# A hybrid encoder block on one core: the residual kept as two half-width tables, with each expert block's rows added by two scatters and the down product taken one half of its columns at a time

## The chip, the core and the metric

The kernel runs on one core of a Trainium2 chip. The metric is the time of one execution on the device in microseconds (us); lower is better. Five engines work side by side, each through its own instructions in order: PE (TensorE, matrix products), ACT (ScalarE), DVE (VectorE), POOL (GpSimd) and SP (SyncE, which here only issues transfers). PEld is PE's loading of the stationary matrix. Sixteen DMA engines carry out the transfers that SP, ACT and POOL issue. Engines wait for each other through semaphores.

## The reference

What is computed is one layer on 2048 tokens of 1024 columns: a mixer (gated recurrence and long convolutions), a residual addition, a mixture of 32 experts of which each token uses two, a second residual addition, and a final norm. The part that the change touches:

```
x = x + y_cat @ w_out[l]
x = x + _hier_moe(_rmsnorm(x, norm_ffn_g[l]), ...)      # top 2 of 32 experts per token

def expert_block(args):                  # 128 tokens of one expert
    xblk, e = args
    a = jax.nn.silu(xblk @ w1[e]) * (xblk @ w3[e])
    return a @ w2[e]                     # 512 -> 1024 columns

y = jnp.zeros((n_tok, d)).at[sorted_tok].add(yb[dest] * sorted_gate[:, None])
return _rmsnorm(x, norm_final_g)
```

## The kernel before

The program is a row of phases (filters and first norm, input projection and recurrence, long convolutions, `output_projection`, `route`, `experts`, `final_norm`). Between two phases all engines meet, and SP clears the next phase's semaphores one by one and adds 16 to those that start from a base (`PhaseSemaphores.begin`); then the phase starts.

`output_projection` works on 16 tiles of 128 tokens. For a tile DVE writes the new residual `X2`, ACT issues its store to the scratch table `X2` in DRAM (L1309) and only then squares the tile for the next norm (L1312); the norm gives `h`, which PE turns and multiplies for the router's logits.

`route` sorts the tokens by expert into blocks of 128. In this run there are 48 blocks for the 32 experts: each expert has one or two.

`experts` loops over experts and, within one, over its blocks (`per_block`: the count is read from memory, so every engine runs the same loops by itself). Float32 products are made of three products of rounded parts (`products`, L1670: high by high, high by low, low by high). For block B:

- SP loads the weights of the next expert, 12 slabs of 128 x 1024 (8 slabs as two transfers of 2 KB rows, 4 slabs of `exp_w2` with 4 KB rows), each as soon as DVE has finished with the slab of the expert before (L1617).
- ACT and DVE split the weights in pairs of slabs (`split_w`: `wh_hi`/`wh_lo` for the up products, `wy_hi`/`wy_lo` for the down product). Each of these engines does so before its own work on the first block of that expert, in its instruction order.
- PE makes the up products of block B (48 matmuls into banks `p1` and `p3`), turns the gathered rows of block B+1 (`px`), makes the down product `y` of the block before (24 matmuls into two banks `pyy0` and `pyy1`, 512 columns each), and turns the activations of the block just done (`pta`).
- ACT in its body: `a_hi` from `pta`, then `store_y` (both halves of the block's result, scaled by the gates, into `yb`), then the silu of the up product, then `x_hi`.
- POOL in its body: `scatter` (wait for `y_evac`, copy the 128 row numbers to `curspot`, add the rows of `yb` to table `X2` by an indirect transfer with add, L1638), then `gather_after` (rows of block B+2 into `xg`, L1625), then `added` (wait until the scatter has landed, tell ACT by `y_added`). ACT overwrites `yb` only after that, so no two scatters are under way at once.

After the loops PE makes one more down product, ACT stores two blocks and POOL scatters them one after the other (L1654 on). `final_norm` loads table `X2` in 16 transfers of 512 KB from SP (L1825), squares and scales each tile on ACT and DVE, and stores each in two transfers (L1831).

Of the kernel before, what the change touches and what calls it, by code (L numbers as in the profile page):

```python
# [11 lines left out]
P = 128  # L12
# [1083 lines left out]
def output_projection(nc, dram, LG, w_hi, w_lo, ident):  # L1096

    NL = N_GROUPS + N_EXP
    with ExitStack() as ctx:
# [171 lines left out]
        def _(act):  # L1271
# [27 lines left out]
            for t in range(NT):  # L1299
# [9 lines left out]
                act.dma_start(dram["X2"][t], X2[:, q, :]).then_inc(x2_out[q], 16)  # L1309
# [8 lines left out]
            for q in range(4):  # L1318
                act.wait_ge(x2_out[q], 16 * (NT // 4))

        @block.vector
        def _(dve):
# [26 lines left out]
            for t in range(NT):  # L1349
# [23 lines left out]
                at_least(dve, x2_out[q], 16 * (t // 4))  # L1373
# [178 lines left out]
def experts(nc, dram, nblk, idx, spot, weight, ident):  # L1552
# [5 lines left out]
    with ExitStack() as ctx:  # L1558
# [18 lines left out]
        pool_passed, act_passed = sem("pool_passed"), sem("act_passed")  # L1577
        xg_in, y_out = sem("xg_in", 0), sem("ye_out", 0)
# [5 lines left out]
        spot_ready, y_added = sem("spot_ready"), sem("y_added")  # L1584
        idx_ready, trx, xhi_ready, xlo_ready = sem("idx_ready"), sem("trx"), sem("xhi_ready"), sem("xlo_ready")
        s_ready, a_ready, tra, ahi_ready, alo_ready, y_done, y_evac = (
            sem(n) for n in ("s_ready", "a_ready", "tra", "ahi_ready", "alo_ready", "y_done", "y_evac"))
# [32 lines left out]
        def _(pool):  # L1620
# [24 lines left out]
            rows = dram["X2"].rearrange("t p d -> (t p) d")  # L1645
# [3 lines left out]
            def body(e, B):  # L1649
                scatter(B)  # L1650
                gather_after(B + 1)
                added(B)

            B = per_block(pool, "pool", body)  # L1654
            for last in range(2):
                scatter(B + last)
# [5 lines left out]
        def _(pe):  # L1662
# [23 lines left out]
            def y(B):  # L1686
# [241 lines left out]
```

## Time and profile before

| | |
|---|---|
| median of 3 runs | 2351.66 us (2348.36 to 2352.35) |
| the profiled execution's own time | 2352.69 us |
| its span in the profile | 2350.9 us |
| phase `experts`, first instruction | 1380.1 us of the span |
| phase `final_norm`, first transfer issued | 2305.95 us of the span |
| granted TensorE clock, mean | 0.946 of full speed |

A row of the profile gives an engine, a line of the kernel, an operation, the tiles it writes and reads (buffer numbers left out, so `pyy` is both banks), its count and its duration. Idle time in front of an instruction is put down to whatever ended it. "PE busy" counts overlapping matmuls, so it can read 100% while the step from one matmul to the next is shorter than the duration given for one.

### The profile page before, as it was taken

The page shows a single profiled execution, that of the slowest core. Times are in us where ns is not written, and L with a number is a line of the kernel's source. Part 1 is how long each engine was busy: PE and PEld are TensorE (multiplying, and loading weights), DVE is VectorE, ACT ScalarE, POOL GpSimd, SP SyncE. Part 2 cuts the span into 40 slices and gives each one's busy share as a digit, 9 for nine tenths or more (in the row PEclk, how much of TensorE's full clock was granted, in tenths as well). Part 3 has the DMA queues.
Part 4 walks back from the last instruction along what each step waited for, and adds up shares of the span by engine and source line. Part 5 has one row for each costly group of instructions (what it writes and reads, how often), then busy time and mean ns, then how long its engine had stood idle before and what let it go on. Part 6 is the DMA issues. An engine that isn't in the chain of part 4 may idle for free. (4 is left out here: it accounts for less than half of the span.)

```text
span 2350.9 us, 30834 instructions
## 1 busy us (share of the span) xinstructions
PE 2076.8 (88%) x9101; PEld 1502.8 (64%) x9102; DVE 1217.1 (52%) x1106; ACT 1142.7 (49%) x1335; POOL 341.4 (15%) x310
## 2 busy tenths in 40 slices
PE   3997999999999497869999459999999999999980
PEld 2655787777666131227778348888787788888870
DVE  7553223224666454654444443555868755654643
ACT  6771222226565232333332134566868766665643
POOL 0560000000000130220000002221211121221220
PEclk9998999999999798989999759999999999999995
DMA  5561213221110698756443157776989987886847
GB/s 186 163 222 58 72 36 99 90 72 39 38 39 18 261 367 324 274 203 230 166 135 103 53 190 221 268 268 217 383 300 375 384 285 227 292 287 195 286 132 303
DMA packets 239628, 462.15 MB, mean 197 GB/s; under 512 B 24896, under 2 KB 87332, under 8 KB 235173
## 3 DMA queue, kind: packets, MB, share of 16 engines
q1 hardware_dynamic: 201798, 375.23, 43.9%
q0 software_dynamic: 14400, 52.44, 9.3%
q10 hardware_dynamic: 23360, 33.56, 4.4%
q8 instruction: 43, 0.70, 0.1%
q14 instruction: 27, 0.22, 0.0%
HBM read 346.86 MB, written 114.29 MB: 196 GB/s over the span
## 5 line engine op out<-in xcount | busy, mean ns | idle before, releaser
L1670 PE MATMUL p<-wh_hi,x_hi 128*128 128x512 f32 x768 | 308.5, 402 | 11.0 <-DVE wh_lo L1792 10.9
L1792 DVE TENSOR_TENSOR wh_lo<-w_raw,wh_hi 128x2048 fp32r<-128x2048 f32 x128 | 284.8, 2287 | 51.6 <-ACT wh_hi L1757 49.8
L1670 PE MATMUL p<-wh_lo,x_hi 128*128 128x512 f32 x768 | 303.8, 396 | 0.0
L1670 PE MATMUL p<-wh_hi,x_lo 128*128 128x512 f32 x768 | 303.7, 395 | 0.0
L495 PE MATMUL pj<-h_hi,wp_hi 128*128 128x512 f32 x640 | 256.5, 401 | 12.4 <-DVE wp_lo L672 12.4
L495 PE MATMUL pj<-h_lo,wp_hi 128*128 128x512 f32 x640 | 253.6, 396 | 0.0
L495 PE MATMUL pj<-h_hi,wp_lo 128*128 128x512 f32 x640 | 253.6, 396 | 0.0
L1757 ACT ACTIVATE wh_hi<-w_raw 128x2048 fp32r<-128x2048 f32 x128 | 234.6, 1915 | 0.2
L1670 PEld LDWEIGHTS p<-wh_hi,x_hi 128*128 128x128 f32 x768 | 144.5, 188 | 49.9 <-DVE wh_lo L1792 15.1
L992 POOL TENSOR_TENSOR arena<-arena 128x512 f32<-128x512 f32 x32 | 56.8, 1776 | 782.9 <-DVE arena L1008 782.9
L1670 PEld LDWEIGHTS p<-wh_hi,x_lo 128*128 128x128 f32 x768 | 144.4, 188 | 35.3
L1670 PEld LDWEIGHTS p<-wh_lo,x_hi 128*128 128x128 f32 x768 | 144.6, 188 | 33.0
L1670 PE MATMUL pyy<-wy_hi,a_hi 128*128 x392 | 159.1, 406 | 2.8 <-ACT yb L1741 2.4
L1670 PE MATMUL pyy<-wy_hi,a_lo 128*128 x392 | 155.0, 396 | 0.0
L1670 PE MATMUL pyy<-wy_lo,a_hi 128*128 x392 | 154.9, 395 | 0.0
L495 PEld LDWEIGHTS pj<-h_hi,wp_hi 128*128 128x128 f32 x640 | 120.7, 189 | 43.3 <-DVE wp_lo L672 13.9
L1792 DVE TENSOR_TENSOR wy_lo<-w_raw,wy_hi 128x2048 fp32r<-128x2048 f32 x64 | 144.0, 2286 | 0.9 <-ACT wy_hi L1757 0.8
L495 PEld LDWEIGHTS pj<-h_lo,wp_hi 128*128 128x128 f32 x640 | 120.7, 189 | 29.4 <-issue 1.0
L495 PEld LDWEIGHTS pj<-h_hi,wp_lo 128*128 128x128 f32 x640 | 120.6, 188 | 29.2
L1803 DVE TENSOR_TENSOR a<-p,s 128x512 f32<-128x512 f32 x48 | 33.2, 692 | 204.7 <-ACT s L1766 180.9
L563 ACT ACTIVATE hraw<-pj 128x512 f32<-128x512 f32 x48 | 28.8, 599 | 217.9 <-PE pj L495 217.9
L1757 ACT ACTIVATE wy_hi<-w_raw 128x2048 fp32r<-128x2048 f32 x64 | 120.3, 1916 | 13.1 <-DMA w_raw<-in_exp_w_dram 7.3
(290 smaller groups left out, 3571.8 us busy)
## 6 DMA issues: line engine op xcount, KB each, us to landing
w_raw<-in_exp_w_dram SPq DMA_DIRECT2D x512, 256.0 KB, 4.9
w_raw<-in_exp_w_dram SPq DMA_DIRECT2D x128, 512.0 KB, 9.5
scratch_KA<-work SPq DMA_DIRECT2D x32, 512.0 KB, 3.0
kin<-scratch_KA SPq DMA_DIRECT2D x32, 512.0 KB, 7.3
arena<-scratch_SA SPq DMA_DIRECT2D x32, 512.0 KB, 6.0
scratch_SI<-arena SPq DMA_DIRECT2D x32, 512.0 KB, 4.1
wp_raw<-in_w_in_dram SPq DMA_DIRECT2D x20, 512.0 KB, 3.8
h_raw<-in_x_dram ACTq DMA_DIRECT2D x4, 2048.0 KB, 19.8
```

The source lines that it names most:

```text
L495: last = pe.matmul(out, w[:, s, k, :], h, start=(k == 0 and i == 0), stop=(k == KC - 1 and i == 2))
L563: ins = act.activation(out[:, 512 * n:512 * (n + 1)], pj[n][:, :], func)
L992: dif = pool.tensor_tensor(yr[:, n % 2, :], by_r[:, n % 2, 0, :], by_i[:, n % 2, 1, :], ALU.subtract)
L1670: mm = pe.matmul(acc[:, :], x[:, k, :], w, start=(k == 0 and i == 0), stop=(k == n - 1 and i == 2))
L1757: act.activation(place, raw[:, j:j + 2, :], ACT.Copy).then_inc(rounded, 1)
L1792: dve.tensor_tensor(lo, raw[:, j:j + 2, :], hi.bitcast(F32), ALU.subtract).then_inc(lowered, 1)
L1803: dve.tensor_tensor(a[:, :], p3[:, :], s1[:, :], ALU.mult).then_inc(a_ready, 1)
```

## The change

The scratch table `X2` (17 tiles x 128 x 1024) becomes two tables `X20` and `X21` of 512 columns. `output_projection` stores a tile with two transfers, `final_norm` loads it with two. In `experts` PE makes all 12 matmuls of the first 512 columns and then the 12 of the second; the first half is signalled by its own semaphore (`half_done`), ACT evacuates each half on its own signal and its own `y_added`, and POOL adds each half with a scatter of its own, 2 KB per row in place of 4 KB. `added` waits for both scatters in turn. Five more semaphores belong to the phase: four that start from a base, and one that starts from zero.

```
@@ output_projection, scalar
-                act.dma_start(dram["X2"][t], X2[:, q, :]).then_inc(x2_out[q], 16)
+                for c in range(2):
+                    act.dma_start(dram[f"X2{c}"][t], X2[:, q, c * 512:(c + 1) * 512]).then_inc(x2_out[q], 16)
@@ experts, gpsimd
-            def scatter(B):
-                pool.wait_ge(y_evac, BASE + B + 1)
-                pool.tensor_copy(cur_spot[:, :], spot[:, ds(B, 1)]).then_inc(spot_ready, 1)
-                pool.wait_ge(spot_ready, BASE + B + 1)
+            def scatter(B, c):
+                pool.wait_ge(y_evac[c], BASE + B + 1)
+                if c == 0:
+                    pool.tensor_copy(cur_spot[:, :], spot[:, ds(B, 1)]).then_inc(spot_ready, 1)
+                    pool.wait_ge(spot_ready, BASE + B + 1)
                 pool.sem_inc(pool_passed, 1)
-                pool.indirect_dma_start(out=rows, out_offset=bass.IndirectOffsetOnAxis(ap=cur_spot[:, :], axis=0),
-                                        in_=yb[:, :], in_offset=None, compute_op=ALU.add).then_inc(y_out, 16)
+                pool.indirect_dma_start(out=rows[c], out_offset=bass.IndirectOffsetOnAxis(ap=cur_spot[:, :], axis=0),
+                                        in_=yb[:, c * 512:(c + 1) * 512], in_offset=None, compute_op=ALU.add).then_inc(y_out[c], 16)
             def added(B):
-                pool.wait_ge(y_out, B * 16 + 16)
-                pool.sem_inc(y_added, 1)
+                for c in range(2):
+                    pool.wait_ge(y_out[c], B * 16 + 16)
+                    pool.sem_inc(y_added[c], 1)
@@ experts, tensor
-                pe.wait_ge(y_evac, BASE + B + 1)
-                for k in range(FT):
-                    if k % 2 == 0:
-                        pe.wait_ge(lowered, BASE + e * PAIRS + H_PAIRS + k // 2 + 1)
-                    for c in range(2):
-                        whi, wlo = (w[:, ds(place + k, 1), c * 512:(c + 1) * 512].rearrange("p a n -> p (a n)") for w in wy)
+                slab = [[w[:, ds(place + k, 1), :].rearrange("p a n -> p (a n)") for w in wy] for k in range(FT)]
+                for c in range(2):
+                    pe.wait_ge(y_evac[c], BASE + B + 1)
+                    pe.sem_inc(pe_passed, 1)
+                    for k in range(FT):
+                        if c == 0 and k % 2 == 0:
+                            pe.wait_ge(lowered, BASE + e * PAIRS + H_PAIRS + k // 2 + 1)
+                        whi, wlo = (w[:, c * 512:(c + 1) * 512] for w in slab[k])
                         mm = products(py[c], a_hi, a_lo, k, whi, wlo, FT)
+                    if c == 0:
+                        mm.then_inc(half_done, 1)
                 mm.then_inc(y_done, 1)
@@ experts, scalar
-                act.wait_ge(y_done, BASE + B + 1)
-                act.wait_ge(y_added, BASE + B)
-                for c in range(2):
-                    copy = act.activation(yb[:, c * 512:(c + 1) * 512], py[c][:, :], ACT.Copy, scale=weight[:, ds(B, 1)])
-                copy.then_inc(y_evac, 1)
+                scale = weight[:, ds(B, 1)]
+                for c, done in enumerate((half_done, y_done)):
+                    act.wait_ge(done, BASE + B + 1)
+                    act.wait_ge(y_added[c], BASE + B)
+                    act.sem_inc(act_passed, 1)
+                    act.activation(yb[:, c * 512:(c + 1) * 512], py[c][:, :], ACT.Copy, scale=scale).then_inc(y_evac[c], 1)
@@ final_norm, sync and scalar
-                sp.dma_start(x[:, t, :], dram["X2"][t]).then_inc(x_in[t], 16)
+                for c in range(2):
+                    sp.dma_start(x[:, t, c * 512:(c + 1) * 512], dram[f"X2{c}"][t]).then_inc(x_in[t], 16)
-                act.wait_ge(x_in[t], 16)
+                act.wait_ge(x_in[t], 32)
```

The order of instructions on PE at the start of the down product, in the kernel before (`ISA` and `REGISTER_ALU` are waits and address arithmetic in PE's instruction queue):

```order
L1670 MATMUL pyy0<-wy_hi,a_hi 128x512
L1670 ISA
L1670 REGISTER_ALU
L1670 MATMUL pyy0<-wy_lo,a_hi 128x512
L1670 ISA
L1670 MATMUL pyy0<-wy_hi,a_lo 128x512
L1670 ISA x2
L1670 MATMUL pyy1<-wy_hi,a_hi 128x512
```

and in the changed kernel:

```order
L1676 MATMUL pyy0<-wy_hi,a_hi 128x512
L1676 ISA
L1676 REGISTER_ALU
L1676 MATMUL pyy0<-wy_lo,a_hi 128x512
L1676 ISA
L1676 MATMUL pyy0<-wy_hi,a_lo 128x512
L1676 ISA x3
L1676 MATMUL pyy0<-wy_hi,a_hi 128x512
```

The fourth matmul now goes on in bank `pyy0` with the next slab, and `pyy1` starts only after twelve matmuls; the number of matmuls and of queue instructions of the down product is the same (24, and 38 with 10 `REGISTER_ALU`).

POOL's queue in the body of a block, before:

```order
L1635 COPY curspot<-spot 128x1
L1638 DMA scratch_X2<-yb,curspot 2176x1024
L1629 ISA
L1630 ISA
L1622 ISA x3
L1622 COPY curidx<-idx 128x1
L1623 REGISTER_ALU
L1625 DMA xg<-scratch_H2,curidx 128x1024
L1642 ISA
```

and in the changed kernel:

```order
L1638 COPY curspot<-spot 128x1
L1641 DMA scratch_X20<-yb,curspot 2176x512
L1641 DMA scratch_X21<-yb,curspot 2176x512
L1631 ISA
L1632 ISA
L1624 ISA x3
L1624 COPY curidx<-idx 128x1
L1625 REGISTER_ALU
L1627 DMA xg<-scratch_H2,curidx 128x1024
L1646 ISA
```

One indirect transfer stands ahead of the gather that was not there, and everything behind it on POOL moves back by it.

## Rows read from the trace of the kernel before

**Rows 1.** The page: busy time and instructions of each engine

```profile
PE 2076.8 (88%) x9101; PEld 1502.8 (64%) x9102; DVE 1217.1 (52%) x1106; ACT 1142.7 (49%) x1335; POOL 341.4 (15%) x310
```

**Rows 2.** Windows: stretch, busy PE, PEld, DVE, ACT, POOL, clock, DMA share, GB/s

```profile
1400.00:1500.00 100.00, 99.69 (x459) 80.89 (x458) 47.35 (x37) 55.79 (x56) 19.57 (x22) 1.00 0.77 250
1600.00:1900.00 300.00, 297.70 (x1365) 240.06 (x1364) 218.74 (x145) 231.73 (x202) 56.85 (x64) 1.00 0.95 333
```

**Rows 3.** Waits in the experts' stretch: total, times, longest

```profile
ACT yb L1741 <- POOLq L1643: 41.2, 17, 8.2
PE pyy L1670 <- ACT yb L1741: 2.4, 1, 2.4
```

**Rows 4.** Timeline of ACT (start, duration) in a block waiting for `y_added`

```profile
2246.80 1.27 ACT L1741 ACTIVATE yb<-pyy,weight 128x512 f32<-128x512 f32 x2 [2.90 <-POOLq L1643]
...
2254.51 0.60 ACT L1766 ACTIVATE s<-p 128x512 f32<-128x512 f32 x1 [5.14 <-PE p L1670]
```

**Rows 5.** Timelines of ACT and PE in a block late on weights

```profile
1862.31 1.92 ACT L1757 ACTIVATE wy_hi<-w_raw 128x2048 fp32r<-128x2048 f32 x1 [1.78 <-DMA w_raw<-in_exp_w_dram]
...
1870.51 0.50 PE L1670 MATMUL pyy<-wy_hi,a_hi 128*128 x1 [0.37 <-issue]
```

**Rows 6.** DMA queue 1, windows 2320:2345 (4 KB rows) and 1404:1410 (2 KB rows)

```profile
q1 hardware_dynamic: 3066, 10.47, 102.7%
...
q1 hardware_dynamic: 1334, 2.43, 105.2%
```

**Rows 7.** Timeline of PE: down product, then output projection

```profile
2239.63 0.39 PE L1670 MATMUL pyy<-wy_hi,a_lo 128*128 x1
...
2242.43 0.40 PE L1670 MATMUL pyy<-wy_hi,a_lo 128*128 x1
...
1290.44 0.39 PE L1221 MATMUL pB<-wo_hi,y_hi 128*128 128x512 f32 x1
...
1293.01 0.39 PE L1221 MATMUL pB<-wo_hi,y_lo 128*128 128x512 f32 x1
```

**Rows 8.** Timelines of POOL and PE: a gather, and who needs its rows

```profile
2256.83 1.00 POOL L1625 DMA_INDIRECT xg<-scratch_H,curidx  x1 [0.79 <-POOL curidx L1622]
...
2272.42 1.04 PE L1678 MATMUL px<-ident,xg 128*128 128x128 f32 x8
```

**Rows 9.** DMA issues, median from issue to landing: last scatter, all gathers

```profile
scratch_X<-yb,curspot POOLq DMA_INDIRECT x1, 6.2
...
xg<-scratch_H,curidx POOLq DMA_INDIRECT x50, 8.3
```

**Rows 10.** DMA queue 0: one scatter alone (2292:2300), one gather alone (2256:2262)

```profile
q0 software_dynamic: 144, 0.52, 43.5%
...
q0 software_dynamic: 144, 0.52, 25.2%
```

**Rows 11.** Timeline of ACT: its last store of `X2`

```profile
1308.77 0.44 ACTq L1309 DMA_DIRECT2D scratch_X<-X  x1
```

**Rows 12.** Timelines around the start of `experts`: last work, first work

```profile
1375.19 0.23 DVE L1549 COPY weight<-pweights 128x68 f32<-128x68 f32 x1 [12.79 <-PE pweights L1457]
...
1380.11 0.19 POOL L1622 COPY curidx<-idx 128x1 int32<-128x1 int32 x1 [94.85 <-POOLq L75]
```

**Rows 13.** Timelines of ACT, PE and POOL behind the last block, then SP

```profile
2280.02 1.26 ACT L1741 ACTIVATE yb<-pyy,weight 128x512 f32<-128x512 f32 x2
...
2281.93 0.50 PE L1670 MATMUL pyy<-wy_hi,a_hi 128*128 x1 [2.44 <-ACT yb L1741]
...
2282.68 1.61 POOL L1638 DMA_INDIRECT scratch_X<-yb,curspot  x1 [0.82 <-POOL curspot L1635]
...
2289.48 1.27 ACT L1741 ACTIVATE yb<-pyy,weight 128x512 f32<-128x512 f32 x2 [8.20 <-POOLq L1643]
...
2292.17 1.59 POOL L1638 DMA_INDIRECT scratch_X<-yb,curspot  x1 [0.81 <-POOL curspot L1635]
...
2305.95 0.34 SPq L1825 DMA_DIRECT2D xfin<-scratch_X  x1
```

More of the change, by code:

```diff
@@ L1318, in _ @@
             for q in range(4):
-                act.wait_ge(x2_out[q], 16 * (NT // 4))
+                act.wait_ge(x2_out[q], 32 * (NT // 4))
         @block.vector
@@ L1372, in _ @@
                     split_b(t + 1)
-                at_least(dve, x2_out[q], 16 * (t // 4))
+                at_least(dve, x2_out[q], 32 * (t // 4))
                 dve.wait_ge(xa_ready, 2 * t + 2)
@@ L1576, in experts @@
         raw_in = [sem(f"raw_in{r}") for r in range(SLABS)]
-        pool_passed, act_passed = sem("pool_passed"), sem("act_passed")
-        xg_in, y_out = sem("xg_in", 0), sem("ye_out", 0)
+        pool_passed, act_passed, pe_passed = sem("pool_passed"), sem("act_passed"), sem("pe_passed")
+        xg_in, y_out = sem("xg_in", 0), [sem(f"ye_out{c}", 0) for c in range(2)]
         rounded, lowered, used = sem("w_rnd"), sem("w_low"), sem("w_used")
-        spot_ready, y_added = sem("spot_ready"), sem("y_added")
+        spot_ready, y_added = sem("spot_ready"), [sem(f"y_added{c}") for c in range(2)]
         idx_ready, trx, xhi_ready, xlo_ready = sem("idx_ready"), sem("trx"), sem("xhi_ready"), sem("xlo_ready")
-        s_ready, a_ready, tra, ahi_ready, alo_ready, y_done, y_evac = (
-            sem(n) for n in ("s_ready", "a_ready", "tra", "ahi_ready", "alo_ready", "y_done", "y_evac"))
+        s_ready, a_ready, tra, ahi_ready, alo_ready, y_done = (
+            sem(n) for n in ("s_ready", "a_ready", "tra", "ahi_ready", "alo_ready", "y_done"))
+        half_done, y_evac = sem("half_done"), [sem(f"y_evac{c}") for c in range(2)]
         def per_block(eng, name, body, start=None, on=lambda e, r: None):
@@ L1631, in gather_after @@
                 gather(B + 1)
-            def scatter(B):
-                pool.wait_ge(y_evac, BASE + B + 1)
-                pool.tensor_copy(cur_spot[:, :], spot[:, ds(B, 1)]).then_inc(spot_ready, 1)
-                pool.wait_ge(spot_ready, BASE + B + 1)
+            def scatter(B, c):
[3 more added lines that the diff above has]
+                    pool.wait_ge(spot_ready, BASE + B + 1)
                 pool.sem_inc(pool_passed, 1)
-                pool.indirect_dma_start(out=rows, out_offset=bass.IndirectOffsetOnAxis(ap=cur_spot[:, :], axis=0),
-                                        in_=yb[:, :], in_offset=None, compute_op=ALU.add).then_inc(y_out, 16)
+                pool.indirect_dma_start(out=rows[c], out_offset=bass.IndirectOffsetOnAxis(ap=cur_spot[:, :], axis=0),
+                                        in_=yb[:, c * 512:(c + 1) * 512], in_offset=None, compute_op=ALU.add).then_inc(y_out[c], 16)
             def added(B):
-                pool.wait_ge(y_out, B * 16 + 16)
-                pool.sem_inc(y_added, 1)
-            rows = dram["X2"].rearrange("t p d -> (t p) d")
+                for c in range(2):
+                    pool.wait_ge(y_out[c], B * 16 + 16)
+                    pool.sem_inc(y_added[c], 1)
+            rows = [dram[f"X2{c}"].rearrange("t p d -> (t p) d") for c in range(2)]
             gather(0)
@@ L1649, in body @@
             def body(e, B):
-                scatter(B)
+                scatter(B, 0)
+                scatter(B, 1)
                 gather_after(B + 1)
@@ L1655, in _ @@
             for last in range(2):
-                scatter(B + last)
+                scatter(B + last, 0)
+                scatter(B + last, 1)
                 added(B + last)
@@ L1792, in split_w @@
                     dve.tensor_tensor(lo, raw[:, j:j + 2, :], hi.bitcast(F32), ALU.subtract).then_inc(lowered, 1)
-            dve.memset(py[0][:, :], 0.0)
+            dve.memset(py[0][:, :], 0.0).then_inc(half_done, 1)
             dve.memset(py[1][:, :], 0.0).then_inc(y_done, 1)
@@ L1878, in build @@
     for name, shape, dt in (("L", [2, P, NT, CH], F32), ("YT", [NT, P, CT, P], F32), ("KA", [2, P, N2, CH], F32), ("SA", [2, P, N2, CH], F32), ("SI", [2, P, N2, CH], F32),
-                            ("H2", [SEQ, D], F32), ("X2", [NT + 1, P, D], F32)):
+                            ("H2", [SEQ, D], F32), ("X20", [NT + 1, P, D // 2], F32), ("X21", [NT + 1, P, D // 2], F32)):
         dram[name] = nc.dram_tensor(f"scratch_{name}", shape, dt, kind="Internal").ap()
```

## The prediction

> **What bounds the kernel now.** I read the page's engine line first, then the busy time by windows, then the waits, and last the timelines of the places where the change lies. The page names PE as the engine to watch: 88% of the span [rows 1]. The windows say where: in the experts' phase PE is busy 99.2 to 99.7% at the full clock, while ACT and DVE have room [rows 2]. The waits show the other side: PE waited once, 2.4 us, for ACT's `yb`; ACT's 41.2 us of waiting for POOL's `y_added`, 17 times, is the wait that this change addresses [rows 3]. A block shows what it costs [rows 4]: ACT waits 2.90 us for the scatter before, evacuates from 2246.80 to 2248.07, and its next urgent work, the silu, comes at 2254.51, after 5.14 us more of waiting for PE. So inside the loops the scatter's latency lies under PE's matmuls, and the change can shorten the time only behind the last block, where nothing covers it.
>
> Two stretches have a second limit, the transfers. From 1600 to 1900, where most experts have a single block, the DMA engines are 95% busy [rows 2], and weights come just in time or late: at 1862.31 ACT has waited 1.78 us for `w_raw`; that passes down ACT's queue, and PE starts its down product after 0.37 us idle [rows 5]. In the final norm the DMA engines are full, 10.47 MB in 25 us or 419 GB/s [rows 6], so that phase lasts as long as its bytes.
>
> **The change, part by part.**
>
> *PE's order.* The same 24 matmuls, in runs of twelve to one bank in place of three. The down product now makes 12 steps in 2242.43 - 2239.63 = 2.80 us, 0.233 each. Output projection already runs twelve to a bank: 11 steps in 1293.01 - 1290.44 = 2.57 us, 0.234 each [rows 7]. Cost 0, at most the rows' difference of 0.0003 us by 1176 matmuls, 0.4 us; there is nothing in it to gain. The second pair of `wy` is wanted six matmuls, 1.4 us, earlier, but DVE splits both pairs ahead of `a_lo`, which the first matmul needs anyway. The wait for the second half's evacuation moves behind the first twelve matmuls, which can only help.
>
> *ACT.* Inside the loops the early signal `half_done` gives nothing: ACT comes to `store_y` behind `a_hi`, which needs `pta`, and PE makes `pta` after both halves. What is new is that the second half may wait for the second scatter, issued one POOL transfer (1.6 us, [rows 13]) after the first. Even if it lands later by all of that, `yb` in [rows 4] ends at about 2249.7 and 4.8 us are left to the silu. Cost 0; from some 5 us of delay on, each further us would be PE's, 17 times.
>
> *POOL.* One more indirect transfer stands in front of the gather. A half-width one is not in the trace. Bounds: 1.6 us again, or half of it, 0.8. I take 1.6, since the count of rows is the same and gather and scatter of equal bytes differ (1.00 and 1.61, [rows 8, 13]), so bytes are not what sets it. Behind it waits the gather: issued at 2256.83, it is needed by PE at 2272.42 [rows 8], 15.6 us later, and lands in 8.3 [rows 9]. 1.6 us more is hidden, up to some 7.
>
> *DMA work per block.* A scatter alone takes 43.5% of 8 us, 3.48 us of all sixteen engines; a gather 25.2% of 6 us, 1.51 us [rows 10]. For 2 KB rows beside 4 KB rows: full engines move 2.43 MB in 6 us, 405 GB/s, against 419 [rows 6], 3.5% more time. On a scatter that is 0.12 us. In the loose stretches it is hidden. In the 300 us from 1600 on, 16 blocks, lateness builds up over a run of single-block experts: after seven to twelve of them 0.8 to 1.4 us, less what little is free. I take **+0.7 us** (bounds 0 and 16 x 0.12 = 1.9).
>
> *Output projection.* Each tile's store is two issues on ACT's queue in front of the square. For 15 tiles PE's work covers it. For the last everything waits behind it: one more issue, 0.44 us [rows 11], and a step of the queue. **+0.5 us** (0.4 to 0.6).
>
> *Semaphores.* Before `experts` SP makes 32 clears and 30 additions; last work to first work takes 1380.11 - 1375.42 = 4.69 us [rows 12], at most 0.076 each. Five more clears and four more additions: **+0.7 us** (0.5 to 0.7), with every engine waiting.
>
> *Final norm.* The loads, 16 x 512 KB = 8.39 MB, take 20.0 us at 419 GB/s and 20.7 at 405 [rows 6]. The engines being full, that is **+0.7 us** (0 to 0.7). Issuing is no limit: SP's first issue takes 0.34 us [rows 13], and 256 KB take 0.63.
>
> *Behind the last block.* Here the chain is bare [rows 13]. Now: `yb` at 2280.02, scatter at 2282.68, landed 6.2 us later [rows 9]; ACT has waited 8.20 us for it [rows 3]; `yb` 2289.48 to 2290.75, POOL's copy and issue 1.4 us, scatter 2292.17, landed 2298.4; the next phase starts at 2305.95. With halves, the first evacuation ends 0.6 us before the pair, so the scatters start at 2282.1 and 2283.7, the second issued by 2285.3. From the end of POOL's work to landing a full scatter takes 6.2 - 1.6 = 4.6 us. For a half I take 2.8: 3.48 us of transfer become 1.74 and the rest stays. Bounds: 2.3 (all of it halves) and 4.6 (nothing does). Landings 2286.5 and 2288.1. PE, which started at 2281.93 and needs 24 steps, is done by 2287.5, so the second evacuation still waits for the landing and, with the 0.4 us of signals that the row has, starts at about 2288.6. POOL passes `added` at 2288.2, needs 1.4 us, scatters 2289.6 to 2291.2 and 2291.3 to 2292.9, and the last rows land at 2295.7 in place of 2298.4: **-2.7 us**.
>
> *Sum.* 0 + 0.7 + 0.5 + 0.7 + 0.7 - 2.7 = -0.1 us. The profiled execution took 2352.69 us, so 2352.6; it stands 1.0 above the median of the runs, so against that I predict **2351.5 us**. What a measurement of this kernel can tell from no change is about 0.2%, 4.7 us.
>
> The Trainium skill speaks against this change: "DMA: Bandwidth & Descriptors", section "Rules for kernel authors", says to coalesce small transfers, and that two transfers to disjoint halves are not worth it, since both run on the same engines. Its section "Anatomy of one DMA — SWDGE (gpsimd) path" puts a transfer at a fixed 2.0 us plus its bytes at 436 GB/s; by that, an estimate, a half lands only 0.6 us sooner than a whole, not 1.8 as taken above, and with two landings in the chain the sum would be +2.3 instead of -0.1. The row of the scatter alone, nearly three times the page's 1.2 us for its 0.52 MB, does not agree with it; no row here shows a half.
>
> **The rivals.**
>
> *A. The forecast*, 2351.5, own range 2349.5 to 2353.5: chance 0.45.
>
> *B. Halves land hardly sooner*, so that the change doesn't do what it says. With 4.6 us for each half the second one of the first pair lands at 2289.9, POOL goes on with copy and two issues to 2294.6, and the last rows land at 2299.2: +0.8 instead of -2.7. The sum is +3.4, 2355.0. For it: part of the 4.6 us may be waiting that does not shrink. Against it: 3.48 us of them are engine time [rows 10]. Chance 0.22.
>
> *C. A half costs POOL half*, 0.8 us. Then the first pair lands by 2286.6, the second evacuation waits for PE instead (2287.6 to 2288.3), the last scatter is issued by 2289.9 and lands at 2292.7: -5.7. The sum is -3.1, 2348.5. Against it: gather and scatter differ at equal bytes [rows 8, 13]. Chance 0.13.
>
> *D. Slower: half-width scatters cost the DMA engines nearly as much as whole ones.* The place is 1600 to 1900, 95% busy [rows 2]: 15 us are free for 16 blocks, 0.9 us each. From 0.9 us more per block on (a half at 2.2 us in place of 1.74) the weights come later and later, and PE waits as in [rows 5]. At the bound, 3.48 us more per block, 56 us meet 15 free ones: +41, 2392. At 1.3 more per block it is +6, and without the tail's gain (-2.7) and with the small terms 2358 to 2360. For it: an adding transfer costs 2.3 times a plain one [rows 10], and part of that may be per row. Against it: plain 2 KB rows cost 3.5% [rows 6]. The looser window (0.77, [rows 2]) would absorb it. Chance 0.14.
>
> The rest, 0.06: ACT held more than 5 us by the second landing, or another pace of PE.
>
> **How the numbers follow.** Within 0.2% (2346.9 to 2356.4): 0.44 of A, 0.18 of B, 0.09 of C, 0.01 of D: 0.72. Slower: 0.13 of D, 0.04 of B, 0.03 of the rest: 0.20. Faster: 0.04 of C, 0.01 of A, 0.03 of the rest: 0.08. The range reaches from C to the mild end of D: 2348.0 to 2358.5.
>
> **What would show it.** PE's steps still 0.233 us and its windows at 99%; ACT waiting for POOL some 17 times, the silu where it was; two scatters 1.6 us apart in front of each gather; the gap before `experts` longer by 0.7 us; behind the last block, the last landing 2.7 us nearer to PE's last matmul; the final norm's loads 0.7 us longer. A DMA share at 1.0 with PE idle before `pyy` between 1600 and 1900 would prove me wrong towards D; a half that lands 6 us after its issue with the queue empty, towards B.

## The result

The changed kernel took 2357.64 us (median of 8 runs, 2355.98 to 2360.03), the kernel before beside it 2352.01 (2348.36 to 2354.79): ratio 1.0023, 95% interval 1.0013 to 1.0034. So it is slower, by 5.6 us or 0.23%, where I had forecast no difference. Its profiled execution took 2360.03 us, span 2358.3, 7.4 above the span before.

Page of after, the row that answers to [rows 1]:

```profile
PE 2082.7 (88%) x9101; PEld 1502.6 (64%) x9102; DVE 1216.7 (52%) x1106; ACT 1143.2 (48%) x1335; POOL 451.9 (19%) x360
```

The same instructions on PE, with 5.9 us more of busy time; POOL has 50 more transfers, as costed. Windows of after, columns as in [rows 2]:

```profile
1400.00:1500.00 100.00, 99.69 (x449) 80.39 (x448) 50.11 (x38) 58.13 (x58) 27.80 (x28) 0.98 0.80 258
1600.00:1900.00 300.00, 297.41 (x1355) 237.56 (x1354) 215.67 (x144) 229.68 (x201) 104.34 (x80) 1.00 0.96 330
```

PE still reads 99%, and the DMA engines went from 0.95 to 0.96 only: rival D, the one that ended on the slower side, did not happen. Yet a stretch of the same length holds 1355 matmuls where it held 1365 (1357 and 1364 in windows moved by 2.5 us). The busy share does not show this: of 300 us, PE is busy in 297.4 with the fewer matmuls and in 297.7 with the more. Waits in the experts' stretch of after, as [rows 3]:

```profile
POOL curspot L1638 <- DMA scratch_X<-yb,curspot: 94.9, 17, 6.3
ACT yb L1753 <- POOLq L1647: 32.3, 25, 6.1
PE pyy L1676 <- DVE a_lo L1796: 2.1, 1, 2.1
```

ACT waits for landings 25 times, where I had forecast some 17, and PE never waits for ACT. So the loss has to be looked for in the steps of PE, from the start of one matmul to the start of the next. Timeline of PE, one block of after (the ninth, block 8): the turn of `x`, the first, fifth to seventh and thirteenth matmul of the down product, `pta`, and the next block's first matmul:

```profile
1559.12 1.03 PE L1684 MATMUL px<-ident,xg 128*128 128x128 f32 x8
1560.06 0.49 PE L1676 MATMUL pyy<-wy_hi,a_hi 128*128 x1
...
1561.12 0.39 PE L1676 MATMUL pyy<-wy_lo,a_hi 128*128 x1
1561.35 0.40 PE L1676 MATMUL pyy<-wy_hi,a_lo 128*128 x1
1561.63 0.50 PE L1676 MATMUL pyy<-wy_hi,a_hi 128*128 x1
...
1563.17 0.39 PE L1676 MATMUL pyy<-wy_hi,a_hi 128*128 x1
...
1565.97 0.60 PE L1689 MATMUL pta<-ident,a 128*128 128x128 f32 x4
1566.52 0.50 PE L1676 MATMUL p<-wh_hi,x_hi 128*128 128x512 f32 x1
```

The same places in the same block before:

```profile
1555.18 1.03 PE L1678 MATMUL px<-ident,xg 128*128 128x128 f32 x8
1556.00 0.50 PE L1670 MATMUL pyy<-wy_hi,a_hi 128*128 x1
...
1558.90 0.40 PE L1670 MATMUL pyy<-wy_hi,a_hi 128*128 x1
...
1561.70 0.60 PE L1683 MATMUL pta<-ident,a 128*128 128x128 f32 x4
1562.28 0.49 PE L1670 MATMUL p<-wh_hi,x_hi 128*128 128x512 f32 x1
```

From `px` to `pyy` 0.94 us instead of 0.82; the first twelve matmuls 3.11 instead of 2.90, with a step of 0.28 at a slab's start (1561.35 to 1561.63); the last twelve 2.80 in both. The loss lies in blocks like this one, 16 of the 47 with a down product, in which `a_lo` comes late, because DVE first splits an expert's weights. Timeline of DVE in the same block of after:

```profile
1556.49 2.28 DVE L1803 TENSOR_TENSOR wy_lo<-w_raw,wy_hi 128x2048 fp32r<-128x2048 f32 x1
1558.70 0.68 DVE L1796 TENSOR_TENSOR a_lo<-pta,a_hi 128x512 fp32r<-128x512 f32 x1
```

`a_lo` ends at 1559.38, 0.26 us after `px` has begun and only 0.68 before the down product. PE's queue waits for it with everything of the down product behind it, so the queue has no work done ahead for the matmuls. What it then has to do is in the trace's records of the queue's own instructions, which the views of the profile leave out (start, duration, instruction, line; `>=` marks a semaphore waited for, `++` one counted). First after, then before, each from the release to the second slab:

```
1559.417 0.051 EVENT_SEMAPHORE L1699  $S[163]>= $S[160]>= $S[111]++
1559.568 0.037 FUSED_REGOPS L1702
1559.663 0.156 FUSED_REGOPS L1676  $S[106]>=
1559.877 0.018 SEQ_ASSERT L1676
1559.954 0.051 FUSED_REGOPS L1676
1560.083 0.018 SEQ_ASSERT L1676
1560.16 0.032 ALU_OP L1676
1560.272 0.018 SEQ_ASSERT L1676
1560.369 0.173 FUSED_REGOPS L1676

1555.478 0.037 FUSED_REGOPS L1693  $S[166]>=
1555.573 0.156 FUSED_REGOPS L1670  $S[108]>=
...
1556.801 0.173 FUSED_REGOPS L1670
```

These are the register operations that turn `place + k` into an address; the one of 0.173 us makes the next slab's place. In the new order it comes after three matmuls, in the old one after six. So the arithmetic of all four slabs now falls within the first twelve matmuls, and one more instruction, the count of `pe_passed` (0.051), stands between the release and the first matmul. A second count stands between the halves, on one record with the wait for the second half's evacuation. Both belong to L1699, and the number of queue instructions given with the change, 38 before and after, is that of the line of the matmuls alone.

By stage, in all traces (us; distances between two rows that every trace has). **OP**: the first `xt` load of output projection to the first load of `route`. **Setup**: last `weight` copy of `route` to first `curidx` copy. **Loops**: first p matmul of block 1 to that of the last block, without the four blocks 22 to 25, which wait for weights in every kernel and are in the next column. **Tail**: last block's first p matmul to the final norm's first load. **Norm**: from there to the end.

| kernel | OP | setup | loops | blocks 22-25 | tail | norm |
|---|---|---|---|---|---|---|
| before | 269.4 | 4.91 | 770.4 | 74.8 | 44.8 | 45.0 |
| after | 270.5 | 5.43 | 774.3 | 75.0 | 41.8 | 47.6 |
| e1 order alone | 269.6 | 4.91 | 771.4 | 75.0 | 45.2 | 45.0 |
| e2 order back | 270.7 | 5.43 | 770.4 | 74.9 | 41.5 | 46.5 |
| e3 side | 270.6 | 5.43 | 770.6 | 75.6 | 40.9 | 45.9 |
| e4 before, side | 269.6 | 4.91 | 770.0 | 74.8 | 44.9 | 45.1 |
| e5 up front | 270.6 | 5.43 | 771.4 | 75.6 | 42.6 | 46.5 |
| e6 before, count | 269.5 | 5.03 | 772.1 | 74.3 | 45.0 | 45.1 |
| e7 before, moves | 270.6 | 4.91 | 770.4 | 74.4 | 45.0 | 47.2 |
| e8 tail | 270.6 | 5.43 | 775.8 | 75.1 | 39.4 | 46.5 |
| e10 tail, order back | 270.7 | 5.43 | 770.3 | 76.2 | 41.4 | 46.9 |
| e11 one issue | 269.8 | 6.45 | 770.3 | 76.6 | 41.4 | 45.8 |
| e12 both | 269.8 | 6.45 | 770.2 | 75.5 | 39.9 | 45.7 |

Each row of the table is one trace. What comes before output projection moved by 1.3 us between before and after and by up to 6 us (1048.2 to 1054.1) over all traces, and block 0 by 1.4 us (19.4 to 20.8), with and without the change alike: in block 0 PE's granted clock is at its lower level, 0.50, for a longer or shorter time (before 0.57 from 1396 to 1400 and 1.00 from there; after 0.50 until 1404 and 0.96 in the 4 us behind). I put no part of the result there.

### The profile page after: what moved, and what is told of

Read it like the earlier page. It is cut to its first block and busy times, and to the rows that moved or that the text cites. A ratio compares the mean times of both kernels' runs of the same rounds, so it can differ in the third digit from the quotient of the medians.

```text
span 2358.3 us, 31173 instructions
## 1 busy us (share of the span) xinstructions
PE 2082.7 (88%) x9101; PEld 1502.6 (64%) x9102; DVE 1216.7 (52%) x1106; ACT 1143.2 (48%) x1335; POOL 451.9 (19%) x360
## 5 line engine op out<-in xcount | busy, mean ns | idle before, releaser
L1803 DVE TENSOR_TENSOR wh_lo<-w_raw,wh_hi 128x2048 fp32r<-128x2048 f32 x128 | 284.8, 2287 | 51.6 <-ACT wh_hi L1768 44.8
L1641 POOL DMA_INDIRECT scratch_X<-yb,curspot x100 | 172.7, 1727 | 58.0 <-POOL curspot L1638 35.7
```

Of the source, the lines that this page charges most:

```text
L1641: pool.indirect_dma_start(out=rows[c], out_offset=bass.IndirectOffsetOnAxis(ap=cur_spot[:, :], axis=0), in_=yb[:, c * 512:(c + 1) * 512], ...
L1803: dve.tensor_tensor(lo, raw[:, j:j + 2, :], hi.bitcast(F32), ALU.subtract).then_inc(lowered, 1)
```

## The experiments

**e1, e2, e3, e4: the loops.** Four theories compete: the arithmetic on PE's queue (1), long runs of matmuls into one bank (2), the wait for the second evacuation in the middle (3), the second scatter (4). e1 is before with only

```diff
-                for k in range(FT):
-                    ...
-                    for c in range(2):
+                for c in range(2):
+                    for k in range(FT):
```

> The kernel before (one table, one scatter, one signal per block) with only PE's order of the change: twelve matmuls into the first bank, then twelve into the second. The measure is the length of the experts' loops, from the first p matmul of the first block to the first of the last: 864.7 us before (1396.47 to 2261.14), 869.9 after (1398.98 to 2268.92). Theory 1, PE's queue: in the new order the address arithmetic of all four slabs falls into the first twelve matmuls, and in blocks where a_lo comes late the queue has no lead; then this kernel shows the loss, loops 868.5 to 870, time +4 to +5 us against before. Theory 2, matmuls into one bank for long run slower: the same here. Theory 3, the wait for the second half's evacuation and the early signal cost it: loops 864.7 to 865.2, time within 1 us. Theory 4, the second scatter (POOL, DMA, writes into memory) costs it: loops 864.7, time the same.

Measured: 1.0006 (0.9997 to 1.0015), 2.2 us above before in the medians where +4 to +5 was expected, so a miss. The loops took 866.9 us, but 1.0 of the 2.2 more lies in block 0; blocks 1 to 46 grew by 1.2 us, a quarter of what theory 1 asked for. The mechanism is there (`pyy` to `pta` is 5.89 us in place of 5.70 in the late blocks, those with a late `a_lo`) but not the size.

e2 is after with PE's order of before. The edit also moves the second wait to the front and takes out both counts of `pe_passed`:

```diff
+                for c in range(2):
+                    pe.wait_ge(y_evac[c], BASE + B + 1)
+                for k in range(FT):
+                    for c in range(2):
                         ...
+                        if k == FT - 1 and c == 0:
+                            mm.then_inc(half_done, 1)
```

> The changed kernel (two tables, two scatters, two evacuation signals) with PE's order of before: each slab's two halves one after the other; both evacuation waits ahead of the first matmul, half_done given at the last matmul of the first half. Theory 1 and theory 2: loops back to 864.7 to 865.5, time 4 to 5 us under the changed kernel, so about +2.5 to +3 against before, what output projection, semaphores, final norm and tail leave. Theory 3: the same, since the mid wait is gone too. Theory 4: loops stay at 869 to 870 and the time at +5.6.

Measured: 1.0006 (0.9997 to 1.0016), in the medians 1.2 us above before where +2.5 to +3 was expected; loops 865.9, and without block 0 as before (770.4 in the table). Two scatters per block cost these blocks nothing: theory 4 is out. What exactly on PE cost it, e2 can't tell, since it takes out three things at once.

e3 is after with the dynamic part of the address taken once; e4 is the same on before:

```diff
-                slab = [[w[:, ds(place + k, 1), :].rearrange(...) for w in wy] for k in range(FT)]
+                side = [w.rearrange("p (r k) n -> p r (k n)", r=2)[:, ds(place, 1), :].rearrange("p r m -> p (r m)") for w in wy]
...
-                pe.reg_mov(place1, r * FT)
+                pe.reg_mov(place1, r)
```

> The changed kernel with PE's new order kept, but the dynamic part of the weight address made once for the side r of wy instead of once per slab (the slab's place in it is a constant), so that the long register operations between the matmuls are gone; the two waits for the wy pairs become one ahead of the first matmul. Theory 1: loops back to 864.5 to 865.5, time about +3 against before. Theory 2 (pace of a bank) and theory 3 (the mid wait, which stays): loops stay at 869 to 870. Theory 4: the same, 869 to 870.

> The kernel before with the same cheaper address. Theory 1: the queue kept up already, with 0.2 us at the start of a late block at most; loops 863.5 to 864.7, time 0 to -1.5 us against before. If loops grow, the single wait for both wy pairs costs something. Theories 2 to 4 expect no change here.

Measured: e3 1.0007 (0.9998 to 1.0016), 1.5 us above before where 3 were expected, loops 865.9; e4 1.0000 (0.9991 to 1.0009), loops 864.6. In e3, with twelve matmuls to a bank and the wait in the middle, the down product of block 8 on PE's timeline is

```profile
1558.69 1.03 PE L1684 MATMUL px<-ident,xg 128*128 128x128 f32 x8
1559.67 0.50 PE L1676 MATMUL pyy<-wy_hi,a_hi 128*128 x1
...
1565.38 0.60 PE L1689 MATMUL pta<-ident,a 128*128 128x128 f32 x4
1565.73 0.48 PE L1676 MATMUL p<-wh_hi,x_hi 128*128 128x512 f32 x1
```

5.71 us, the full pace: theory 2 is out, twelve matmuls in a row to one bank are no slower. Theory 3 is out as the main cause too, since the wait in the middle is still there and the loops are back. But `px` to `pyy` is still 0.98 here, where it was 0.82 before, so something else stands in front.

**e5, e6: the count.** e5 is after with the first edit, e6 before with the second:

```diff
                 for c in range(2):
                     pe.wait_ge(y_evac[c], BASE + B + 1)
-                    pe.sem_inc(pe_passed, 1)
+                for c in range(2):
                     for k in range(FT):
...
                 pe.wait_ge(y_evac, BASE + B + 1)
+                pe.sem_inc(pe_passed, 1)
```

> The changed kernel with both evacuation waits ahead of the first matmul and without the two counts of pe_passed; PE's new order, two tables and two scatters stay. Measure: blocks 1 to 46, from the second block's first p matmul to the last block's, since block 0 differs from run to run: 845.2 us before, 849.4 after, 846.4 with the order alone, 845.3 with the order put back. Theory 1 as mended by the first runs: the new order costs 0.19 us in the down product of a late block, and the count of pe_passed costs 0.15 us before it, because the wait for a_lo now sits on a queue instruction of its own with all the address arithmetic behind it; without the counts this kernel comes to 846.2 to 846.7, px to pyy is 0.79 again, pyy to pta stays 5.9. Rival: the second scatter's work costs the other 3 us; then 849.

> The kernel before with one more queue instruction on PE, a count of pe_passed behind the wait for y_evac, and nothing else. Mended theory 1: px to pyy becomes 0.94 in the sixteen blocks with a late a_lo and stays 0.79 in the others; the late blocks are 18.30 and 18.55 us, blocks 1 to 46 take 847.0 to 847.8. Rival (one instruction is nothing, the wait in the middle costs it): 845.2.

Measured: e5 1.0015 (1.0006 to 1.0025), e6 1.0002 (0.9992 to 1.0011). The late blocks do in the traces what was expected; e5 has 0.80, 5.89 and blocks of 18.35 and 18.39 us. Blocks 1 to 46 took 847.0 in e5 and 846.4 in e6, 0.3 above and 0.6 below the ranges; blocks 22 to 25, late on weights, differ by over 1 us between the two. In time e5 gained nothing that can be told against after, though its loops are 2.9 us shorter: its stages add up to +1.6 us by the means at the end of this document, at the low end of its interval (+1.4 to +5.9). For the loops the traces decide here, not the times. e6, block 8:

```profile
1557.56 1.04 PE L1678 MATMUL px<-ident,xg 128*128 128x128 f32 x8
1558.52 0.50 PE L1670 MATMUL pyy<-wy_hi,a_hi 128*128 x1
...
1564.23 0.60 PE L1683 MATMUL pta<-ident,a 128*128 128x128 f32 x4
1564.80 0.49 PE L1670 MATMUL p<-wh_hi,x_hi 128*128 128x512 f32 x1
```

One count on the queue, recorded with 0.051 us, made 0.94 to 0.96 of the 0.79 to 0.82 in the late blocks outside 22 to 25 and nothing in the others. The Trainium skill, "Perfetto Trace Analysis", section "Sequencer-only Instruction (DRAIN, etc)", says that the profile shows only the execution of such an instruction, not its fetch, decode and push; this trace agrees, with 0.15 us from the start of the count's record of 0.05 to the next record.

Means of the late blocks outside 22 to 25, six followed by a block of the same expert and seven by one of the next (us):

| kernel | px to pyy | pyy to pta | same expert next | other expert next |
|---|---|---|---|---|
| before (e2 and e10 within 0.02) | 0.80 | 5.70 | 18.16 | 18.40 |
| e1, e5: arithmetic early | 0.80 | 5.89 | 18.35 | 18.39 |
| e6: one count | 0.94 | 5.70 | 18.30 | 18.52 |
| after: both, two counts | 0.94 | 5.89 | 18.49 | 18.68 |
| e3: two counts, cheap address | 0.96 | 5.70 | 18.32 | 18.31 |
| e4: no count, cheap address | 0.91 | 5.70 | 18.27 | 18.27 |

Where the same expert follows, 0.19 for the arithmetic and 0.15 for the first count add up. Where another follows, PE's queue itself seems to set the period. There the block grows by 0.12 us for one count (e6), by 0.28 for the two of after, by nothing for arithmetic that only stands elsewhere, and it is shorter than before when the arithmetic is gone. Part of the 0.96 of e3 seems to be its earlier wait for both pairs of `wy`, since e4 has 0.91 with that wait and no count. Together 6 x 0.33 + 7 x 0.28 = 3.9 us, against 774.3 - 770.4 = 3.9. By the loops of e5 (771.4) 1.0 of it is the order of the arithmetic and 2.9 are the counts with the wait in the middle. How much of the 2.9 is the second count and how much the wait on the same record stays open: no run has one without the other.

**e7: the transfers outside.** Before, with each store and load of `X2` made as two halves of one table:

```diff
-                act.dma_start(dram["X2"][t], X2[:, q, :]).then_inc(x2_out[q], 16)
+                for c in range(2):
+                    act.dma_start(dram["X2"][t][:, c * 512:(c + 1) * 512], X2[:, q, c * 512:(c + 1) * 512]).then_inc(x2_out[q], 16)
```

> The kernel before, in which only the stores of output projection and the loads of the final norm are made as two transfers of 512 columns each, on one table; the experts' phase is untouched. As forecast: output projection +0.5, final norm +0.7. By the traces of the changed kernel and of the first runs (final norm 49.1, 48.0 and 47.5 us with halves, 47.1 three times without; output projection 274.5 with halves, 273.3, 274.6 and 273.6 without): final norm 47.5 to 49, output projection 274.5, time +1 to +3 us against before. Rival: they differ by chance, then 47.1 and no difference.

Measured: 1.0014 (1.0005 to 1.0024): the moves alone make the kernel slower by a measurable amount, in the medians by 4.7 us where +1 to +3 was expected. OP +0.9 over the mean of six kernels with single stores (269.65), norm +2.1 over theirs (45.1). Timeline of ACT in after at the last tile, to be put beside [rows 11]:

```profile
1310.14 1.27 ACTq L1310 DMA_DIRECT2D scratch_X<-X  x2
1311.52 1.06 ACT L1313 ACTIVATE junk<-X 128x1024 f32<-128x1024 f32 x1 [1.10 <-issue]
```

The second issue of the pair takes 0.83 us more, not 0.44; e7 has the same 1.27 for its pair.

**e8, e10: POOL's order in the tail.** e8 is after with, behind the loops,

```diff
-            for last in range(2):
-                scatter(B + last, 0)
-                scatter(B + last, 1)
-                added(B + last)
+            scatter(B, 0)
+            scatter(B, 1)
+            for c in range(2):
+                pool.wait_ge(y_out[c], B * 16 + 16)
+                pool.sem_inc(y_added[c], 1)
+                scatter(B + 1, c, last_spot)
+            added(B + 1)
```

> The changed kernel, in which behind the loops POOL issues the last block's first scatter as soon as the first half of the block before has landed, in place of waiting for both halves. In the changed kernel ACT evacuates the last block's first half at 2295.17 and POOL scatters it only at 2299.68, behind the second half's landing at 2298.2. If POOL's waiting for both is what kept the tail's gain away: first scatter at about 2297.0, second at 2299.8, the last landing 1.5 to 2 us nearer to the last block, time 1.5 to 2 us under the changed kernel. If the landings under way are slowed by each other: less than 0.8 us.

Measured: 1.0019 (1.0010 to 1.0029). The tail shrank by 2.4 us against after, a little more than expected, but the time did not fall by the 1.5 to 2 us expected. The loops are 1.5 us longer: the 29 blocks with an early `a_lo` outside 22 to 25 take 18.42 us in place of 18.37 (from the first p matmul to `px` it is 11.33 to 11.35 us in place of 11.29 to 11.31 in all blocks). The new index tile stood ahead of `xg`, `x_hi` and the rest. e10 has it behind all others, and PE's order of before.

> The changed kernel with PE's order of before (e2_order_back) and the tail of e8_tail; the second index tile stands behind all others, so that no tile is moved. In e8_tail it stood in front and moved every later tile by 32 bytes; there the blocks with an early a_lo took 18.435 us in place of 18.375. Expected: blocks 1 to 46 in 845.2 to 845.5 us, the other blocks at 18.375 again (if the shift is the cause; 18.43 if the new tail or chance is), the way from the last block to the next phase 37.8 us as in e8_tail (39.9 in e2_order_back, 42.7 before). Time 1 to 3 us under e2_order_back, that is -1.5 to +0.5 us against before.

Measured: 1.0001 (0.9992 to 1.0010), loops 770.3, the early blocks at 18.37 again: the place of the tile had been the cause, since the new tail is here too and PE's order alone had left these blocks at 18.37 in after and e2. But the tail is 41.4, not 39.4 as expected. By PE's order of before, the last block's first half is not ready until the whole product is. Timeline of ACT:

```profile
2292.45 0.69 ACT L1756 ACTIVATE yb<-pyy,weight 128x512 f32<-128x512 f32 x1 [7.81 <-PE pyy L1680]
2294.49 0.69 ACT L1756 ACTIVATE yb<-pyy,weight 128x512 f32<-128x512 f32 x1 [1.35 <-POOLq L1665]
```

**e11, e12.** e11 is e10 with both tables in one tensor, each tile stored and loaded by one transfer of 2 KB rows; POOL makes the second table's indices before the loops. e12 is e11 with the new order in the very last down product alone:

```diff
-                    act.dma_start(dram[f"X2{c}"][t], X2[:, q, c * 512:(c + 1) * 512]).then_inc(x2_out[q], 16)
+                act.dma_start(dram["X2"][:, t].rearrange("c p d -> p c d"), X2[:, q, :].rearrange("p (c d) -> p c d", c=2)).then_inc(x2_out[q], 16)
...
-            y(per_block(pe, "pe", body, on=on))
+            y(per_block(pe, "pe", body, on=on), halves=True)
```

> e10_tail_back with both tables in one tensor, so that a tile's store and its load are one transfer each (rows still of 2 KB); the second table's indices are made once before the loops. Tells the number of issues from the row size: by the issues, output projection falls from 274.5 to 273.4 us and the final norm from 48.3 (mean of six) to 47.1; by the 2 KB rows the norm stays at 47.8 or above. Time 1 to 2.5 us under e10_tail_back, so about -2 us against before (-4 to 0).

> e11_one_issue with PE's new order in the very last down product alone, behind the loops, where no address arithmetic is in anyone's way: the loops keep the order of before. If the tail's gain needs the early first half as well as POOL's order, the way from the last block to the next phase falls from 39.8 to about 37.8 us and the time is some 2 us under e11, 2350 to 2351, -0.5 to -3.5 us against before. If e8's 37.8 came from something else (a landing that happened to be quick), it stays at 39 to 40.

Measured: e11 1.0002 (0.9993 to 1.0011), e12 0.9995 (0.9986 to 1.0004). With these edits the two tables cost nothing that can be told, where the changed kernel cost 5.6 us; e12 is no measurable gain either. OP is 269.8 and the norm 45.8 and 45.7: on average over the traces the second issues had cost 0.8 us in OP and 0.9 in the norm, and the 2 KB rows 0.7 in the norm. The 1 to 2.5 us that e11 was to gain on e10 are not there in time: making the indices lengthens the setup from 5.43 to 6.45 and eats half of it. The tail of e12 is 39.9, 1.4 us less than that of e11, where 2 were expected.

**e9, e13: POOL's drain.** Before, with one and with ten more gathers at POOL's very end (their rows are not used):

```diff
             pool.wait_ge(xg_in, B * 16 + 32)
             pool.sem_inc(pool_passed, 1)
+            for more in range(10):
+                pool.indirect_dma_start(out=xg[:, :], out_offset=None, in_=dram["H2"], in_offset=...).then_inc(xg_in, 16)
+                pool.wait_ge(xg_in, B * 16 + 48 + 16 * more)
+                pool.sem_inc(pool_passed, 1)
```

> The kernel before with one more gather and a wait for it at the very end of POOL's work in the experts' phase. It asks what sets POOL's drain at the phase's end, 5.04 us in every trace of a kernel with one scatter per block and 2.14 us in every one with two. If it is set by the kind or the row size of the last scatter, it stays near 5.0 or becomes another fixed value below it; if it is set by how many indirect transfers there were (100 and 150 so far), one more moves it by a few hundredths at most; if by the last transfer's kind, a plain gather changes it by over 1 us.

> The kernel before with ten more gathers at the very end of POOL's work in the experts' phase, each waited for. With one more (e9_b_drain) the drain went from 5.036 to 5.117 us. If it goes by the number of transfers it becomes about 5.84 us, or falls by several us if a ring of descriptors starts anew in between; if 5.117 was chance or a plain gather's fixed value, it stays at 5.1.

Single runs, 2358.01 and 2407.06 us; only the drain is asked. The traces' records of the drain (start, duration) in before (100 indirect transfers in the phase), e9 (101), e13 (110) and after (150):

```
2298.64  5.036 GpSimd DRAIN
2303.87  5.117 GpSimd DRAIN
2351.53  5.852 GpSimd DRAIN
2306.79  2.137 GpSimd DRAIN
```

Each gather added at the end lengthened the drain by 0.081 us (0.816 for ten). That is no price for every transfer of the phase, since 100 x 0.081 would be 8.1 and not 5.04, and after, with 150, has less. A count that starts anew somewhere would fit both, but no run shows one, and the transfers of after differ in width too.

## Why the prediction was wrong

The forecast was 2351.5 us, no change, and the kernel became slower. The time, 2357.64, lies inside the range of 2348.0 to 2358.5 by luck: the range reached so high for rival D, and the reason was not among the rivals.

**PE's order, "Cost 0 ... there is nothing in it to gain": this step failed.** It compared the pace of matmuls [rows 7], and that comparison was right (e3). It left out what stands between them on PE's queue. My list of the change on PE counted matmuls and waits; the count of `pe_passed` was read as nothing and the register operations were not looked at. The step put at 0 cost 3.9 us, 1.0 for the arithmetic and 2.9 for the counts and the wait in the middle (after against e5). That wait "can only help", I had said: PE had waited for ACT once in the whole phase, so there was hardly anything to gain by moving it. "The rest", 0.06, held "another pace of PE" without a mechanism.

**ACT and POOL.** Right: PE does not wait for ACT, and a half scatter costs POOL the whole price (1.59 and 1.56 us), which stays hidden. Rival C is out.

**DMA per block.** +0.7 forecast. Blocks 22 to 25, those late on weights, took 75.5 us on average over eight kernels with half scatters (74.9 to 76.6; after itself 75.0) and 74.7 over seven with whole ones (74.3 to 75.0): +0.9. What the forecast rested on was sized too small: DMA queue 0 of after from 2292 to 2300, a pair of halves, beside [rows 10]:

```profile
q0 software_dynamic: 288, 0.52, 51.9%
```

4.15 us of the engines against 3.48: +0.67 per block, not 0.12. That is three quarters of the way to where rival D begins (0.9). That this makes the 0.9 us of blocks 22 to 25 is likely and not shown by a run of its own.

**Output projection.** +0.5 forecast, +1.0 measured (270.6 over seven kernels with pairs, 269.65 over six without): the second issue of a pair takes 0.83 us.

**Semaphores.** +0.7 (0.5 to 0.7) forecast, 5.43 - 4.91 = +0.5 measured.

**Final norm.** +0.7 forecast, +1.6 measured on average. The size of the rows' part was right (e11, e12: +0.7), but not the picture of a phase that "lasts as long as its bytes". ACT's timelines show what sets it, the square of the second tile, which waits for its load (before, then after):

```profile
2313.02 1.06 ACT L1840 ACTIVATE junk<-xfin 128x1024 f32<-128x1024 f32 x1 [2.65 <-DMA xfin<-scratch_X]
...
2319.74 1.06 ACT L1852 ACTIVATE junk<-xfin 128x1024 f32<-128x1024 f32 x1 [4.55 <-DMA xfin<-scratch_X]
```

Counted from the first load's issue, that square starts at 7.07 us before and at 9.03 in after. From it to the last tile's square it is 20.27 us in both, and from it to the end 37.9 to 38.0 us in the kernels with 4 KB rows (38.4 in e13) and 38.5 to 38.6 in those with 2 KB rows. So the start of this one square, and 0.6 us more for 2 KB rows, make the length of the phase. The square starts at 7.0 to 7.2 us with whole loads, at 7.3 and 7.4 with one issue of 2 KB rows (e12, e11), and at 7.4 to 9.0 with pairs. "Issuing is no limit" was wrong here: SP's last issue for the second tile starts 1.80 us after its first one in after and 0.87 before, 0.9 us later, as much as pairs cost on average. Why single traces with pairs differ by up to 1.6 us stays open.

**Tail.** -2.7 forecast, -3.4 measured on average (41.6 over the six kernels without the edits of e8 and e12 against 45.0 over five). The number came near by luck, since the gain has another source. Timelines of ACT, POOL and SP in after, to be read beside [rows 13]:

```profile
2287.81 1.26 ACT L1753 ACTIVATE yb<-pyy,weight 128x512 f32<-128x512 f32 x2
2295.17 0.69 ACT L1753 ACTIVATE yb<-pyy,weight 128x512 f32<-128x512 f32 x1 [6.09 <-POOLq L1647]
2298.35 0.69 ACT L1753 ACTIVATE yb<-pyy,weight 128x512 f32<-128x512 f32 x1 [2.50 <-POOLq L1647]
...
2289.85 1.59 POOL L1641 DMA_INDIRECT scratch_X<-yb,curspot  x1 [0.79 <-ACT yb L1753]
2291.75 1.56 POOL L1641 DMA_INDIRECT scratch_X<-yb,curspot  x1 [0.30 <-issue]
...
2301.56 1.55 POOL L1641 DMA_INDIRECT scratch_X<-yb,curspot  x1 [0.30 <-issue]
...
2310.71 0.81 SPq L1837 DMA_DIRECT2D xfin<-scratch_X  x2
```

The first half landed 4.9 us after its issue, 3.3 behind the end of POOL's work: I had taken 2.8, between 2.3 and 4.6. The second, under way beside it, landed 6.4 us after its issue, 4.8 behind POOL's work. With the last pair's 5.0 (DMA view of after, 2299 to 2308) the last rows landed at 2306.6, 37.6 us into the last block, against 2298.4 or 37.2 before: nothing gained, which is where rival B ends (+0.8), though not each half came as late as it assumed. What shortened the tail is the way from there to the final norm, 4.1 us in place of 7.6, and 2.9 of it is POOL's drain (2.14 us in place of 5.04), which I had not seen as a term.

By an estimate from the Trainium skill's "DMA: Bandwidth & Descriptors", section "Anatomy of one DMA — SWDGE (gpsimd) path", a half would land 0.6 us sooner than a whole. This trace does not agree: the first half of a pair came 6.2 - 4.9 = 1.3 sooner, with the second already issued behind it. And the rule against two transfers that the prediction quotes from that page is written for halves of the partitions; here the columns are halved.

Over all traces: OP +1.0, setup +0.5, loops +3.9, blocks 22 to 25 +0.9, tail -3.4, norm +1.6, together +4.5; the runs say +5.6 with an interval of some 3.1 to 8.0. The same terms give sums inside the intervals of e1 to e8 and e10 to e12 too. The single profiled execution's 7.4 holds 1.3 us from before output projection and 1.1 from block 0.

## What to carry to other kernels

When a loop around matmuls is turned, look at what is computed between them on the queue: an address with a dynamic part belongs outside the loop over its constant part (e3). An instruction between a late release and the first matmul counts with its whole step on the queue (e6); whether the wait can be put behind the arithmetic was not tried. Both mattered here only in the blocks where the queue is released late. A PE that reads 99% busy can still be limited by its queue, and the steps between starts show it where shares don't. And halving transfers is not free where they are issued one behind the other in front of work, even when each engine has room.

## What the runs showed of the hardware

- A semaphore count on PE's queue, recorded with 0.051 us, takes 0.15 us of the queue (e6).
- POOL's drain at the end of the phase took 5.036 us after 100 indirect transfers, 5.117 after 101 and 5.852 after 110 (before, e9, e13), and 2.137 after the 150 of after. What sets it is open.
- Two adding scatters of 2 KB rows cost the DMA engines 19% more than one of 4 KB rows (4.15 against 3.48 us), and POOL twice as much (1.59 and 1.56 us against 1.59).
- The second of two stores issued one behind the other by ACT took 0.83 us more, where a single one takes 0.44 (after, e7). On SP the second issue of a pair of loads took 0.43 (after).
- Moving the tiles from `xg` on by 32 bytes cost 0.05 us in each block with an early `a_lo`, 1.5 us in all (e8 against after and e10). Which of the tiles does it wasn't tried.
